# Attention keys turned by their own products, in a two-layer hybrid decoder trunk

## The chip, the cores and the metric

The kernel runs on one core of one Trainium2 chip. The metric is the time of the whole program on the device, in microseconds (us), as a median of runs. A core has five engines that work side by side and meet at semaphores: PE (matrix products; its weight loads are listed as PEld), DVE (vector), ACT (scalar), POOL (GpSimd) and SP (which here only issues DMAs).

## The reference

A trunk of two layers on 256 tokens of width 1024. Layer 0 mixes tokens with multi-head latent attention, then has a dense SwiGLU; layer 1 has an RG-LRU block, then a top-2-of-8 expert SwiGLU. Only attention is touched. Cut to that:

```python
lat = h @ w_in                                  # 1024 -> 384 + 256 + 32
c_q, c_kv, k_rope = split(lat, [384, 640])
c_q, c_kv = rmsnorm(c_q, q_norm), rmsnorm(c_kv, kv_norm)
q  = (c_q @ w_uq).reshape(B, S, 16, 64 + 32)    # q_nope, q_rope
kv = (c_kv @ w_ukv).reshape(B, S, 16, 64 + 64)  # k_nope, v
q_rope, k_rope = apply_rope(q_rope), apply_rope(k_rope)   # one k_rope for all heads
s = (q_nope @ k_nope.T + q_rope @ k_rope.T) * scale       # per head, causal, blocks of 128 queries
o = softmax(s) @ v                              # then @ w_o, residual, and the rest of the trunk
```

## The kernel before

All products of attention's projections are made in three passes of a split float32 (`hi`: rounded to the fast format, `lo`: the rest): `sh*mh`, `sh*ml`, `sl*mh`, three matmuls for each pair of operands (`product`, L431 to L445). A weight unit of 128 rows lands by DMA in `raw`, ACT makes its `w_hi` (`split_hi`), DVE its `w_lo` (`split_lo`). Tokens lie in two tiles of 128 (`TT` = 2).

*Projections.* The normed latents are turned once to `c_hi`, `c_lo` (latent by token). `up_projection` makes q in six units of (token tile, 512 columns): the turned latents of one token tile are the stationary operand (128x128), 512 columns of weight move. The result lies tokens on partitions; ACT copies it to `q` (`q_copy`). Keys and values come together in eight units in the same way, in the order `KV_ORDER`: one unit has four heads of one token tile, 64 columns of key and 64 of value for each head. Each unit's bank is copied in two instructions, the key columns to `k[:, t, head, 0:64]` and the value columns to `v`; ACT copies units 0 to 5, DVE units 6 and 7. GpSimd rotates the 32 columns `k_rope` of each tile (`rope`, six small instructions a tile), then the queries of tile 0, then copies the rotated key part into all 16 heads of `k`, once a tile. DVE rotates the queries of tile 1.

*Heads.* PE's program runs over 16 heads with stages shifted against each other. In step i it turns head i (`transpose_qk`), makes the scores of head i-1 (two matmuls), turns the probabilities of head i-4 (three transposes) and, every second step, multiplies probabilities by values for two heads (`values`). Units 5, 6 and 7 of keys and values stand in steps 0, 1 and 4 (`UP_BETWEEN`). `transpose_qk` is four transposes into one PSUM bank:

```python
for n, src in enumerate([q[:, 0, h], q[:, 1, h], k[:, 0, h], k[:, 1, h]]):
    mm = pe.transpose(psum[0:QK, h % 2, n * P:(n + 1) * P], src, ident[:])
```

In step i ACT copies the turned head (`qk_copy`, 96 partitions x 512 columns into `qkT`, which lies in `gain_mla`), copies the turned probabilities of head i-4 (`pT_copy`), makes the two exponentials of head i-2 (`exps`, L919), and every second step the high half of an output (`o_high`). DVE normalizes head i-3 (L2053 to L2055: a reciprocal and two scalings), makes the maxima of head i-1 with the mask added (L2044, L2047), and every second step the low half of an output (`o_low`, L2060), which waits for `o_high`. PSUM banks and `qkT` are double, by h % 2; the scores of head h wait for the maxima of head h-2. After the last head the output projection runs, whose first parts are already woven between the last heads; then the dense layer.

The order on each engine is written out by hand, and each engine takes its instructions in that order. The copy helper of ACT is L828, so all its copies carry that line; the three matmuls of `product` are L441 to L443; transposes of heads are L1305, scores L1316 and L1317, transposes of probabilities L1326, values L1341 and L1345.

SP issues all weight loads in one queue; ACT and GpSimd issue a few small DMAs of their own.

## Time and profile before

| | |
|---|---|
| median of 3 runs | 1304.98 us (1304.45 to 1305.43) |
| profiled execution, its own time | 1304.9 us |
| span of the trace | 1303.1 us |
| PE busy | 1298.2 us, 100% of the span |
| DVE busy | 649.2 us, 50% |
| ACT busy | 287.8 us, 22% |
| GpSimd busy | 86.9 us, 7% |
| granted PE clock | 1.00 of full speed |
| attention, from the first latent transposes to the last head | about 23 to 87 us |
| experts (L1663) | 67% of the chain that ended last |

The trace is of one execution. Its span begins with the first instruction and ends with the last; the program's own time holds some 1.8 us more around it. A group "x2" is two instructions in a row, merged; the difference of two start times tells how long the engine was held, which is less than the duration printed, since the end of one instruction overlaps the start of the next. A bracket at the end of a row gives the idle time before it and who ended it.

### The profile page before, as it was taken

What the parts mean: (1) busy time and instruction counts of PE and PEld (TensorE: products, weight loads), DVE (VectorE), ACT (ScalarE), POOL (GpSimd) and SP (SyncE); (2) the same over time, 40 slices, a digit from 0 to 9 for tenths busy, and PEclk for the clock granted to TensorE, in tenths of its full rate; (3) what the DMA queues carried; (4) which work ended last, traced back from release to release, by engine and by line L of the source; (5) the groups of instructions that cost most, each with busy time, mean ns of one, the idle gap of its engine ahead of it and who ended that gap; (6) DMA issues with size and microseconds to landing.
All of it is one profiled execution on the core that took longest, in us unless ns stands there. A gap on an engine that the chain in (4) does not pass through costs nothing.

```text
span 1303.1 us, 25215 instructions
## 1 busy us (share of the span) xinstructions
PE 1298.2 (100%) x10760; PEld 852.5 (65%) x10760; DVE 649.2 (50%) x1471; ACT 287.8 (22%) x432; POOL 86.9 (7%) x116
## 2 busy tenths in 40 slices
PE   9999999999999999999999999999999999999998
PEld 5878888888997444555555555555555555555555
DVE  5888666666887344233433533423343353342436
ACT  4874444433694000010010010001001001000102
POOL 3401111111002110000000000000000000000100
PEclk9999999999999999999999999999999999999999
DMA  8625555556369999999999999999999999999992
GB/s 304 253 105 173 193 192 193 193 193 210 120 249 378 358 416 406 421 409 414 419 408 416 419 420 405 419 419 405 405 420 410 403 420 421 411 413 419 419 411 101
DMA packets 124423, 441.92 MB, mean 339 GB/s; under 512 B 7346, under 2 KB 18052, under 8 KB 109732
## 3 DMA queue, kind: packets, MB, share of 16 engines
q1 hardware_dynamic: 119696, 424.57, 82.5%
q0 software_dynamic: 4560, 15.85, 3.4%
q8 instruction: 81, 1.33, 0.4%
q14 instruction: 18, 0.15, 0.0%
q10 hardware_dynamic: 68, 0.02, 0.0%
HBM read 430.84 MB, written 9.57 MB: 338 GB/s over the span
## 4 chain that ended last, share of the span: by engine, by line
PE 98%; ACT 1%; DMA 1%; SPq 0%; issue 0%; DVE 0%
PE psum L1663 67%; PE psum L441 9%; PE psum L443 8%; PE psum L442 8%; PE psum L1210 1%; PE psum L1669 1%; DMA raw<-in_mla_w_in 1%; PE psum L1317 0%; ACT w_hi L412 0%; PE psum L1305 0%; PE psum L1326 0%; PE psum L1341 0%; PE psum L1316 0%; PE psum L1615 0%; PE psum L1428 0%; PE psum L457 0%
## 5 line engine op out<-in xcount | busy, mean ns | idle before, releaser
L1663 PE MATMUL psum<-raw_more,hT 128*32 128x512 f32 x1656 | 535.7, 592 | 0.0
L1663 PE MATMUL psum<-raw,hT 128*32 128x512 f32 x1032 | 334.6, 592 | 0.0
L1663 PE MATMUL psum<-raw_more,xg_odd 128*32 128x512 f32 x1680 | 245.4, 592 | 0.0
L1663 PE MATMUL psum<-raw_more,xg 128*32 128x512 f32 x1704 | 241.8, 592 | 0.1
L2473 DVE STREAM_TRANSPOSE hT<-hid 32x128 f32<-32x128 f32 x672 | 206.2, 307 | 10.3
L2463 DVE SCALAR_TENSOR_TENSOR hid<-hid,psum 96x512 f32<-96x512 f32 x55 | 37.6, 683 | 302.7 <-PE psum L1663 301.9
L1154 ACT ACTIVATE hid<-psum 96x1024 f32<-96x1024 f32 (+1 forms) x32 | 29.2, 914 | 663.8 <-PE psum L1663 474.2
L1663 PEld LDWEIGHTS psum<-raw_more,hT 128*32 128x32 f32 x1656 | 154.3, 110 | 32.0 <-issue 32.0
L1663 PEld LDWEIGHTS psum<-raw_more,xg_odd 128*32 128x32 f32 x1680 | 84.5, 110 | 98.0 <-issue 98.0
L1663 PEld LDWEIGHTS psum<-raw_more,xg 128*32 128x32 f32 x1704 | 83.4, 110 | 98.2 <-issue 97.8
L1663 PE MATMUL psum<-raw,xg_odd 128*32 128x512 f32 x1008 | 147.7, 592 | 0.0
L1663 PE MATMUL psum<-raw,xg 128*32 128x512 f32 x984 | 144.2, 592 | 0.0
L2450 DVE SCALAR_TENSOR_TENSOR hid<-hid,psum 96x1024 f32<-96x1024 f32 (+1 forms) x32 | 34.7, 1083 | 200.7 <-ACT hid L1154 200.7
L418 DVE TENSOR_TENSOR w_lo<-raw,w_hi 128x2048 fp32r<-128x2048 f32 (+1 forms) x52 | 117.4, 2276 | 26.4 <-ACT w_hi L412 26.4
L412 ACT ACTIVATE w_hi<-raw 128x2048 fp32r<-128x2048 f32 (+1 forms) x60 | 111.4, 1891 | 17.1 <-PE psum L443 16.7
L1663 PEld LDWEIGHTS psum<-raw,hT 128*32 128x32 f32 x1032 | 95.4, 110 | 22.7 <-issue 22.5
L1663 PEld LDWEIGHTS psum<-raw,xg_odd 128*32 128x32 f32 x1008 | 50.7, 110 | 58.8 <-issue 58.8
L441 PE MATMUL psum<-w_hi,xTh_ffn 128*128 128x512 f32 x224 | 87.3, 390 | 0.0
L443 PE MATMUL psum<-w_hi,xTl_ffn 128*128 128x512 f32 x224 | 87.2, 389 | 0.0
L442 PE MATMUL psum<-w_lo,xTh_ffn 128*128 128x512 f32 x224 | 87.2, 389 | 0.0
L1663 PEld LDWEIGHTS psum<-raw,xg 128*32 128x32 f32 x984 | 49.5, 110 | 57.3 <-issue 57.3
L828 ACT ACTIVATE y_main<-psum 32x512 f32<-32x512 f32 x48 | 28.4, 592 | 145.1 <-PE psum L1663 145.1
(368 smaller groups left out, 1352.6 us busy)
## 6 DMA issues: line engine op xcount, KB each, us to landing
raw_more<-in_moe_w_gate SPq DMA_DIRECT2D x71, 1024.0 KB, 18.4
raw_more<-in_moe_w_up SPq DMA_DIRECT2D x70, 1024.0 KB, 18.6
raw_more<-in_moe_w_down SPq DMA_DIRECT2D x69, 1024.0 KB, 17.7
raw<-in_moe_w_down SPq DMA_DIRECT2D x43, 1024.0 KB, 18.0
raw<-in_moe_w_up SPq DMA_DIRECT2D x42, 1024.0 KB, 17.5
raw<-in_moe_w_gate SPq DMA_DIRECT2D x41, 1024.0 KB, 18.3
raw<-in_ffn_w_gate SPq DMA_DIRECT2D x14, 1024.0 KB, 5.2
raw<-in_ffn_w_up SPq DMA_DIRECT2D x14, 1024.0 KB, 5.3
```

Source lines behind the costliest of these rows:

```text
L412: act.activation(w_hi[:, s, 0:width], raw[:, s, 0:width], ACT.Copy).then_inc(hi_done[s], 1)
L418: eng.tensor_tensor(w_lo[:, s, 0:width], raw[:, s, 0:width], w_hi[:, s, 0:width].bitcast(F32), ALU.subtract).then_inc(lo_done[s], 1)
L441: pe.matmul(out_ap, sh, mh, start=first, stop=False, **lone)
L442: pe.matmul(out_ap, sh, ml, start=False, stop=False, **lone)
L443: mm = pe.matmul(out_ap, sl, mh, start=False, stop=last, **lone)
L828: return act.activation(dst, src, ACT.Copy)
L1154: act.activation(hid[:, 0:WIDTH[m] * BANK].rearrange("p (a b) -> p a b", b=BANK), psum[SLOT_ROWS, 0:WIDTH[m]], ACT.Tanh, scale=0.5).then_i ...
L1210: mm = pe.matmul(psum[rows_q, 4 + 2 * t + b, 0:LAT // 2], xT_in[:, a, c0:c0 + 32], unit(raw, s, LAT)[:, a % 3, b * LAT // 2:(b + 1) * LAT ...
L1663: return pe.matmul(psum[rows_q, bank, cols], stationary, moving, start=start, stop=stop, tile_position=(0, rows_q.start), skip_group_check ...
L2450: dve.scalar_tensor_tensor(out=h, in0=h, scalar=1.0, in1=psum[SLOT_ROWS, 0:WIDTH[m]], op0=ALU.add, op1=ALU.mult).then_inc(m_mid, 1)
L2463: dve.scalar_tensor_tensor(out=hid[:, cols], in0=hid[:, cols], scalar=0.5, in1=psum[SLOT_ROWS, BANK_U[h]], op0=ALU.mult, op1=ALU.mult).the ...
L2473: ins = dve.transpose(hT[QUARTERS[to], H_BUF[j], :, QUARTERS[b]].rearrange("p (h r) s -> p h r s", r=2), hid[QUARTERS[b], h * BANK:(h + 1) ...
```

## The change

Keys no longer come with tokens on partitions. A unit of keys takes a 128x128 piece of the key weights (two heads x 64) as the stationary operand and moves the turned latents of both token tiles (256 columns) past it; the product is the turned key of two heads. A PSUM bank holds two such products, four heads. Values come as before, in units of their own of 512 columns. So of the eight units, 0, 1, 6, 7 are keys (12 matmuls of 256 columns each) and 2 to 5 are values (6 of 512). To have key and value columns apart, ACT's and DVE's splits of the two weight units write them reordered, in two instructions of half the width each.

The turned keys are copied to `kT` (heads 4 to 15) and `kT_first` (heads 0 to 3), two copies of 64 partitions x 512 columns a unit: units 0 and 1 by ACT, 6 and 7 by DVE. The rotated part is turned once on PE (`turn_key_rope`, two transposes, before the query unit t = 1, b = 1), copied once by ACT into partitions 64 to 95 of head 0 (`key_rope`, before the last query copy) and spread to the other 15 heads by three DMAs from SBUF to SBUF that ACT issues there. GpSimd's two copies into the heads are gone, and its scratch areas are elsewhere. In the heads PE turns only q, and ACT copies 256 columns in place of 512 to `qT`. The scores wait, for head 0, also for the three DMAs, and for heads 8 and 12 for DVE's copies. Three semaphores are merged with others.

```diff
-                rope(t, kr, kr, 1, areas(t, 1))
+                rope(t, kr, kr, 1).then_inc(roped, 1)
+                pool.wait_ge(roped, t + 1)
...
-            for t in range(TT):
-                pool.tensor_copy(k[:, t, :, NOPE:QK],
-                                 latent[:, t, QR + KVR:LAT].unsqueeze(1).broadcast_to([P, HEADS, ROPE])
-                                 ).then_inc(qk_ready, 1)
...
+            def key_rope():
+                act.wait_ge(c_ps, 2 * TT + 1)
+                copy(kT_first[0][NOPE:QK, 0], psum[0:ROPE, 1, T:2 * T]).then_inc(q_copied, 1)
+                act.wait_ge(q_copied, KEY_ROPE)
+                for dst, n in ((kT_first[0][NOPE:QK, 1:2], 1), (kT_first[1][NOPE:QK], 2), (kT[NOPE:QK], HEADS - 4)):
+                    act.dma_start(dst, kT_first[0][NOPE:QK, 0:1].broadcast_to([ROPE, n, T])
+                                  ).then_inc(x_first_then_rope, 16)
...
+                    if t == TT - 1 and b == 1:
+                        key_rope()
...
-            split_hi(act, mla_use(W_UKV), UKV)
-            split_hi(act, mla_use(W_UKV + 1), UKV)
+            for a in range(KVR // P):
...
+                for w in range(2):
+                    ins = act.activation(keys_first(w_hi, s)[:, w], by_head(raw, s)[:, w], ACT.Copy)
+                ins.then_inc(hi_done[s], 1)
...
-                copy(qkT[0:QK, h % 2, :], psum[0:QK, h % 2, :]).then_inc(qkT_ready, 1)
+                copy(qT[0:QK, h % 2, :], psum[0:QK, h % 2, 0:T]).then_inc(qkT_ready, 1)
...
+            def turn_key_rope():
+                pe.wait_ge(roped, TT)
+                for t in range(TT):
+                    mm = pe.transpose(psum[0:ROPE, 1, T + t * P:T + (t + 1) * P], latent[:, t, QR + KVR:LAT],
+                                      ident[:])
+                mm.then_inc(c_ps, 1)
...
+                if KV_UNITS[n][0] == KEYS:
+                    for e in range(2):
+                        g = 2 * KV_UNITS[n][1] + e
+                        terms = []
+                        for a, (s, _) in enumerate(w_units):
+                            pair = [w[:, s, g * P:(g + 1) * P] for w in (w_hi, w_lo)]
+                            terms.append((pair[0], pair[1], c_hi[:, k0 + a, :], c_lo[:, k0 + a, :]))
...
-                for n, src in enumerate([q[:, 0, h], q[:, 1, h], k[:, 0, h], k[:, 1, h]]):
-                    mm = pe.transpose(psum[0:QK, h % 2, n * P:(n + 1) * P], src, ident[:])
+                for t in range(TT):
+                    mm = pe.transpose(psum[0:QK, h % 2, t * P:(t + 1) * P], q[:, t, h], ident[:])
...
+                    pe.wait_ge(q_copied, 3 * TT + 1)
+                    pe.wait_ge(x_first_then_rope, 16 * 4)
+                if h in (8, 12):
+                    pe.wait_ge(kv_copied_v, KV_COPIED[4 + h // 4])
...
+                pe.matmul(psum[:, 2 + h % 2, P:3 * P], s[:, P:2 * P], keys(h),
                           start=True, stop=True).then_inc(score_ps, 1)
...
+                for e in range(2):
+                    dve.tensor_copy(key_pairs(KV_UNITS[n][1], e),
+                                    psum[e * NOPE:(e + 1) * NOPE, KV_BANKS[n]].rearrange("p (g t) -> p g t", t=T)
+                                    ).then_inc(kv_copied_v, 1)
```

## Rows read from the trace of the kernel before

**Rows 1.** Part 4 of the page: shares of the chain that ended last.

```profile
PE 98%; ACT 1%; DMA 1%; SPq 0%; issue 0%; DVE 0%
```

**Rows 2.** Window 70 to 80 us: PE, PEld, DVE, ACT, POOL busy, clock, DMA.

```profile
70.00:80.00 10.00, 10.00 (x101) 7.85 (x103) 9.13 (x48) 9.96 (x35) 0.00 (x0) 1.00 0.01 2
```

**Rows 3.** PE timeline in the heads: start us, us, line, operation, shapes.

```profile
70.36 0.38 PE L1305 MATMUL psum<-ident,k 128*96 128x128 f32 x2
70.57 0.39 PE L1316 MATMUL psum<-gain_mla 96*128 96x128 f32 x2
...
71.23 0.49 PE L1326 MATMUL psum<-ident,res 128*128 128x128 f32 x3
```

**Rows 4.** ACT timeline in the same pair of heads.

```profile
71.60 0.37 ACT L828 ACTIVATE xTh_mla<-psum 128x256 fp32r<-128x256 f32 x1
71.87 0.58 ACT L828 ACTIVATE gain_mla<-psum 96x512 f32<-96x512 f32 x1
72.34 0.48 ACT L828 ACTIVATE early<-psum 128x384 f32<-128x384 f32 x1
```

**Rows 5.** DVE timeline in the same pair of heads.

```profile
68.57 0.15 DVE L2053 RECIPROCAL res<-res 128x2 f32<-128x2 f32 x1
...
70.23 0.16 DVE L2053 RECIPROCAL res<-res 128x2 f32<-128x2 f32 x1
...
72.00 0.42 DVE L2060 TENSOR_TENSOR xTl_mla<-psum,xTh_mla 128x256 fp32r<-128x256 f32 x1
72.34 0.15 DVE L2053 RECIPROCAL res<-res 128x2 f32<-128x2 f32 x1
```

**Rows 6.** PE timeline, matmuls at an even pace: first and last of two stretches.

```profile
41.07 0.39 PE L441 MATMUL psum<-w_hi,xTh_mla 128*128 128x512 f32 x1
...
46.96 0.39 PE L443 MATMUL psum<-w_hi,xTl_mla 128*128 128x512 f32 x1
...
379.83 0.28 PE L441 MATMUL psum<-xTh_lru,w_hi 128*128 128x256 f32 x1
...
383.91 0.28 PE L442 MATMUL psum<-xTl_lru,w_hi 128*128 128x256 f32 x1
```

**Rows 7.** ACT timeline: last query copy, last copy of v, first turned head.

```profile
40.59 0.60 ACT L828 ACTIVATE q<-psum 128x512 f32<-128x512 f32 x1 [1.44 <-PE psum L443]
...
48.67 0.38 ACT L828 ACTIVATE xn_mla<-psum 128x256 f32<-128x256 f32 x1
48.94 0.59 ACT L828 ACTIVATE gain_mla<-psum 96x512 f32<-96x512 f32 x1
```

**Rows 8.** PE timeline: a query product of tile 1; the first scores.

```profile
36.31 0.39 PE L441 MATMUL psum<-w_hi,xTh_mla 128*128 128x512 f32 x1
...
49.58 0.49 PE L1316 MATMUL psum<-gain_mla 96*128 96x128 f32 x2
```

**Rows 9.** DVE timeline: maxima of head 1, normalizing of head 2.

```profile
53.36 0.29 DVE L2044 CUSTOM_DVE_ANT_0 res<-psum,mask 128x128 f32<-128x128 f32 x1 [0.69 <-PE psum L1317]
...
58.66 0.17 DVE L2053 RECIPROCAL res<-res 128x2 f32<-128x2 f32 x1
```

**Rows 10.** GpSimd timeline: the last step of each key rotation.

```profile
32.17 0.22 POOL L720 TENSOR_TENSOR res<-k,res 128x16 f32<-128x16 f32 x1
...
33.73 2.35 POOL L720 TENSOR_TENSOR res<-k,res 128x16 f32<-128x16 f32 x1
```

**Rows 11.** Issues on the ACT queue; 1 MB loads, median us to landing.

```profile
0.80 0.60 ACTq L832 DMA_DIRECT2D q<-in_norm_mix  x1
1.44 0.25 ACTq L833 DMA_DIRECT2D q<-in_positions  x1
...
raw<-in_mla_w_o SPq DMA_DIRECT2D x4, 1024.0 KB, 9.4
```

**Rows 12.** End of the heads: scores of head 15; normalizing of head 11.

```profile
78.37 0.39 PE L1316 MATMUL psum<-gain_mla 96*128 96x128 f32 x2
...
76.11 0.15 DVE L2053 RECIPROCAL res<-res 128x2 f32<-128x2 f32 x1
```

More of the change, by code:

```diff
@@ L83, in trunk @@
                 xn_mla = sb(s, "xn_mla", [P, TT, D], F32)
+                with ExitStack() as s2:
+                    attn_area = sb(s2, "attn_area", [P, 2 * KT, T], F32)
                 xTh_mla = sb(s, "xTh_mla", [P, KT, T], F32R)
@@ L166, in trunk @@
         xT_in = early[:, 2].rearrange("p (k t) -> p k t", t=T)
-        k_row = k[:, 1].rearrange("p h c -> p (h c)")
-        gain_col, x_sumsq, x_rstd = k_row[:, 0:KT], k_row[:, 8:8 + TT], k_row[:, 12:12 + TT]
+        gain_col, x_sumsq, x_rstd = kT[:, 6, 0:KT], kT[:, 6, 8:8 + TT], kT[:, 6, 12:12 + TT]
+        kT_rest = kT.rearrange("p (g e) t -> p e g t", e=2)
+        kT_first = [attn_area[:, n + 5:n + 7] for n in (KT, 0)]
         rope_scratch = [gain_mla[:, n * 256:(n + 1) * 256].rearrange("p (h c) -> p h c", c=HALF) for n in range(3)]
         gain_rows = q[0:KT, 0].rearrange("p h c -> p (h c)")[:, 2 * P:3 * P]
-        rows = k[:, 0].rearrange("p h c -> p (h c)")[:, 0:P]
+        rows = kT[:, 0, 0:P]
         angle_area = q[:, 1].rearrange("p h c -> p (h c)")
@@ L179, in trunk @@
         rope_area = res[:, 1, LAT:LAT + HEADS * HALF].rearrange("p (h c) -> p h c", c=HALF)
-        qkT = gain_mla.rearrange("p (b n) -> p b n", b=2)
+        qT = gain_mla[:, 0:2 * T].rearrange("p (b n) -> p b n", b=2)
+        rope_areas = [attn_area[:, n + KT - 1].rearrange("p (h c) -> p h c", c=HALF) for n in (0, KT)]
         v = xn_mla
@@ L187, in trunk, with keys, key_pairs @@
         Q_BANKS = [(4, 5, 2), (6, 7, 3)]
-        KV_BANKS = [(0, 4, 6, 6), (1, 5, 7, 7)]
-        KV_ORDER = [(t, b) for b in range(4) for t in range(TT)]
+        KV_BANKS = [0, 1, 4, 5, 6, 7, 6, 7]
+        KEYS, VALUES = 0, 1
+        KV_UNITS = [(KEYS, 0), (KEYS, 1), (VALUES, 0, 0), (VALUES, 1, 0), (VALUES, 0, 1), (VALUES, 1, 1),
+                    (KEYS, 2), (KEYS, 3)]
         KV_SCALAR = 6
+        KV_COPIED = [2, 4, 5, 6, 7, 8, 2, 4]
+        KEY_ROPE = 6
+        def keys(h):
+            return kT[0:QK, h - 4] if h >= 4 else kT_first[h % 2][0:QK, h // 2]
+        def key_pairs(n, e):
+            return kT_rest[0:NOPE, e, 2 * n - 2:2 * n] if n > 0 else kT_first[e][0:NOPE]
         hT_f = xn_ffn[:, 0, 0:4 * P].rearrange("p (a b) -> p a b", b=P)
@@ L706, in _, with rope @@
             pool.wait_ge(trig_ready, 1)
-            def rope(t, src, dst, width, areas):
+            def rope(t, src, dst, width):
                 sin = trig[:, 0, t].unsqueeze(1).broadcast_to([P, width, HALF])
@@ L712, in rope @@
                 x1, x2 = src[:, :, 0:HALF], src[:, :, HALF:ROPE]
-                a, b, c = areas
+                a, b, c = [area[:, 0:width] for area in rope_areas + [rope_area]]
                 pool.tensor_tensor(a, x1, cos, ALU.mult).then_inc(pool_link, 1)
@@ L1289, in _ @@
                         transpose_latents(1)
+                    if t == 1 and b == 1:
+                        turn_key_rope()
                     up_projection(W_UQ, QR // P, 0, Q_BANKS, q_ps, t, b)
             def up_kv(n):
-                up_projection(W_UKV, KVR // P, QR // P, KV_BANKS, kv_ps, *KV_ORDER[n])
+                if n in KV_BANK_FREE:
+                    pe.wait_ge(*KV_BANK_FREE[n])
+                w_units = [mla_use(W_UKV + a) for a in range(KVR // P)]
+                units = dict(enumerate(w_units)) if n == 0 else {}
@@ new lines, in up_kv @@
+                k0 = QR // P
+                if KV_UNITS[n][0] == KEYS:
+                    for e in range(2):
[4 more added lines that the diff above has]
+                            terms.append((pair[0], pair[1], c_hi[:, k0 + a, :], c_lo[:, k0 + a, :]))
+                        marks = {}
+                        if e == 1 and n == len(KV_UNITS) - 1:
+                            marks = {a: used[s] for a, (s, _) in enumerate(w_units)}
+                        elif e == 1:
+                            marks = {len(terms) - 1: kv_ps}
+                        product(pe, psum[:, KV_BANKS[n], e * T:(e + 1) * T], terms, marks=marks,
+                                units=units if e == 0 else {})
+                else:
+                    _, t, b = KV_UNITS[n]
+                    tok = slice(t * P, (t + 1) * P)
+                    terms = []
+                    for a, (s, _) in enumerate(w_units):
+                        vals = [w[:, s, HEADS * NOPE + b * BANK:HEADS * NOPE + (b + 1) * BANK] for w in (w_hi, w_lo)]
+                        terms.append((c_hi[:, k0 + a, tok], c_lo[:, k0 + a, tok], vals[0], vals[1]))
+                    product(pe, psum[:, KV_BANKS[n]], terms,
+                            marks={len(terms) - 1: kv_ps})
@@ L1999, in _ @@
             c_low(1)
-            for n in range(W_UKV, W_O):
-                split_lo(dve, mla_use(n), UKV)
+            for a in range(KVR // P):
+                s, n = mla_use(W_UKV + a)
+                dve.wait_ge(hi_done[s], n)
+                for w in range(2):
+                    ins = dve.tensor_tensor(keys_first(w_lo, s)[:, w], by_head(raw, s)[:, w],
+                                            keys_first(w_hi, s)[:, w].bitcast(F32), ALU.subtract)
+                ins.then_inc(lo_done[s], 1)
             def rope_queries(t):
```

92 lines of the change are left out of this document (45 added, 47 removed).

## The prediction

> **What bounds the kernel now.** I read the chain that ended last first: it is PE for 98% of the span [rows 1]. A change in attention therefore pays in full only if PE is what attention waits for, and attention is where I looked next. In a window over the heads PE is busy throughout, at the full clock, but ACT is busy 9.96 of 10 us and DVE 9.13 [rows 2]. So PE is first by very little, and the question is how soon another engine takes over. The timelines give that. For two heads DVE goes through the reciprocal of one head at 68.57, of the next at 70.23, an `o_low` at 72.00, and the next pair begins at 72.34 [rows 5]. The period of a pair is 72.34 - 68.57 = 3.77 us. The first head took 1.66. The second took 1.77, because its `o_low` waited for ACT's copy of the same bank, which runs 71.60 to 71.97 [rows 4, 5]. `o_low` itself holds DVE 0.34. Without that wait DVE needs 1.66 + 1.66 + 0.34 = 3.66 us a pair, and I see no other gap in it. DVE's instructions in the heads are not touched by the change. The most that a head can win is thus (3.77 - 3.66) / 2 = 0.055 us, whatever PE saves.
>
> **The change, part by part.**
>
> *PE in the heads.* Two transposes of k per head go: they take 70.57 - 70.36 = 0.21 us [rows 3], over 16 heads 3.4 us. The pair falls from 3.77 to about 3.35 on PE. ACT's copy of the turned head shrinks from 512 columns (72.34 - 71.87 = 0.47) to 256 (like the one of 71.60 to 71.87, 0.27) [rows 4], 0.20 a head: 3.37 a pair. Both are now under DVE's 3.66, so DVE sets the pace.
>
> *PE outside the heads.* Key units: 4 units of 12 matmuls at 256 columns in place of 4 of 6 at 512. At an even pace 26 steps lie between 41.07 and 46.96, 0.227 each; 34 steps between 379.83 and 383.91, 0.120 each, and those reload 128 x 128 weights every time too [rows 6]. Thus 48 x 0.120 = 5.76 against 24 x 0.227 = 5.45, +0.3 us, 0.08 a unit; a unit takes 1.44. The two transposes of the rotated key part add 0.21. PE's own balance is 3.4 - 0.3 - 0.2 = 2.9 us.
>
> *The wait for the rotated keys.* PE now turns them before the matmuls that began at 36.31 [rows 8], and in order, so everything behind it on PE would stand. GpSimd's last addition for them ran 33.73 to 36.08: 2.35 us for a step that takes 0.22 next to it at 32.17 [rows 10]. It stood beside a 128x2048 subtraction on DVE, and the change cuts these into two of half the width. Even unchanged it ends 0.2 us before PE needs it. Cost 0; if it slipped, PE would pay 1:1. The Trainium skill ("SBUF — State Buffer", SBUF: two separate sides) says that DVE with two SBUF inputs and GpSimd exclude one another for a whole instruction; the 2.35 agrees, and by it halves of a DVE instruction free GpSimd about 1.2 us sooner. The two GpSimd copies of k's rotated part also go; they ran while PE was busy with the units of k and v, and take nothing off the path.
>
> *ACT before the first head.* Here ACT holds the path: the first scores start at 49.58 [rows 8], right after the copy of turned head 0 that began at 48.94 [rows 7]. Whatever ACT gets more before it, PE gets too.
> - `key_rope`: one copy (0.27), a wait for its own end (0.1, my estimate), and three DMA issues, which on this queue took 0.25 and 0.60 [rows 11]. ACT stood idle 1.44 us before the last query copy at 40.59 [rows 7], and that hides the first 1.44 of it. The sum is 1.1 to 2.2 us; with 0.4 an issue, near the middle, 1.57. Cost +0.1, bounds 0 and +0.75. Queued behind it are the last query copy, the split of W_O, DVE's rotation of the queries, the unit copies: all of the ramp.
> - Copies of units 0 and 1: two of 512 columns each (0.47 [rows 4]) in place of two of 256 (0.27 [rows 7]): 4 x 0.20 = +0.8. The 64 partitions do not shorten them; the row gives time by columns. Units 2, 3, 4: one of 0.47 in place of two of 0.27: 3 x -0.07 = -0.2.
> - The splits in two halves and in pieces of 64 columns: the copies of k and v already read such pieces, and the one of 48.67 to 48.94 takes the 0.27 of a plain copy of 256 columns [rows 4, 7]. Two fixed parts more, about 0.07 each (0.27 less 256 columns at 0.20), hide in the wait for weights and for PE before the query copies. Cost 0, at most +0.15.
> - The copy of head 0: -0.2.
> Sum: 0.1 + 0.8 - 0.2 - 0.2 = +0.5, so the first scores start at 50.1.
>
> *From there to head 2.* PE: scores 0.66 [rows 3], unit 6 1.44, so 52.2. DVE copies it in two of 512 columns. A DVE pass over 256 holds it 0.34; with the same fixed 0.07, 512 take 0.61. It is done at 53.4. Before, it was done sooner and DVE stood until the maxima of head 1 at 53.36 [rows 9]: the idle time swallows this one. Scores 1 are ready at 53.2. Then maxima and normalizing twice, 2 x 1.66, to 56.7; unit 7 (done on PE at about 56.4, from the same steps) copied in 1.22, to 57.95; maxima 0.88: normalizing of head 2 starts at 58.85 against 58.66 [rows 9], +0.2. From here DVE has no idle time.
>
> *DVE's run.* From there to the normalizing of head 11 at 76.11 [rows 12] lie 9 heads and 4 `o_low`: 17.45 us now, 9 x 1.66 + 4 x 0.34 = 16.3 then. It starts at 58.85 + 16.3 = 75.15, 1.0 us sooner; the next one at 76.8.
>
> *PE's last head.* The scores of head 15 started at 78.37 [rows 12], with PE itself late: 2.26 us after DVE's 76.11. Now PE waits for DVE instead: it needs the maxima of head 13, at 76.8, and before it the turning of head 11's probabilities (0.65 of normalizing and about 0.33 of turning after 75.15) and three matmuls of projection with their start (3 x 0.227 + 0.1), to 76.95. That is 1.4 us sooner. Behind it PE is busy without a wait to the end of the projection, and its work there is unchanged: between the turnings of two heads' probabilities it has projection and values for some 1.7 to 2 us, and DVE needs 1.66 to 2.0 a head, so DVE, ahead by then, stays ahead (it has head 12 at 77.45, head 13 at 79.1, head 14 at 81.1). The 1.4 us reach the end, since PE is the chain afterwards.
>
> *Transfers.* 15 heads x 32 KB, issued at 39.5 to 40.7, needed at 50.1. The nearest row is the loads of 1 MB in attention, 9.4 us from issue to landing [rows 11]: landing at 50.1, just in time. I take it as hidden, since these transfers stand on another queue and hold half as much, and the 9.4 holds the queueing of loads behind one another. The row does not exclude a wait, so it is a rival. The Trainium skill ("DMA: Bandwidth & Descriptors", Queues, rings and completion order, and Anatomy of one DMA) lets the DMA engines alternate between queues, with a fixed 2 us; by that an estimate is 2.0 + 0.48 MB at half of 436 GB/s = 4.2 us, landing near 45. No row here shows two queues at once under load.
>
> **Sum.** -1.4 us on the span of 1303.1. The profiled execution took 1304.9 with what lies around it, 0.1 below the median of 1304.98. So 1303.5 on its own time, 1303.6 as a median.
>
> **The rivals.**
> - *PE's saving comes in full.* If DVE's steps pack closer than 1.66 once PE and ACT wait for them, and the ramp's +0.5 is idle time elsewhere, PE's balance of 2.9 us comes off: 1302.0. For: PE is 98% of the chain. Against: DVE's steps wait for one another's results and show no gap. Chance 0.14.
> - *The ramp eats it.* Issues of 0.60 each cost 0.75 in place of 0.1, and the `o_low` wait stays for a part of the pairs (0.11 each, 0.5 over the run): -1.4 + 0.65 + 0.5 = -0.2: 1304.8. For: ACT holds the ramp. Chance 0.19.
> - *The spread rows land late* (the other side). Scores of head 0 wait for the third transfer, in order, with all heads behind. At 50.1 it begins to cost; it undoes the gain from 51.5, and is slower by over 0.2% from 54.1, 13.4 us after the last issue. At 15 us it is 55.7: +5.6 - 1.4 = +4.2, 1309.2. For: 9.4 us for loads then. Against: they queue behind their own kind. Chance 0.08.
> - The forecast: 0.59.
>
> **Numbers.** A measurement here tells about 0.2%, 2.6 us, from no change: 1302.4 and 1307.6. The first rival lies just beyond it, and the low flank of the forecast (bounds 0 in place of +0.1 and a DVE step shorter by 0.05, -0.9 over the run) a little: faster 0.16. Slower is the last rival, 0.08. The rest, 0.76, within. The range goes from the first rival, 1302.0, to 1305.8, which takes in the second and the landing up to 52.3.
>
> **What would show it.** DVE with no idle time between the normalizing of head 2 and head 15, and a pair of heads in 3.66 us; PE's busy share in the same window down to 9 of 10, and ACT's too; the first scores at 50.1 after a wait for ACT, not for a DMA; 256-column key matmuls at 0.120; DVE's copies of units 6 and 7 at 0.6 each; no PE wait at 36.3 for GpSimd. It is wrong if the pair takes 3.77 still (PE or ACT had more hidden work), if scores 0 wait for a transfer, or if key matmuls run slower than those of the later layer.

## The result, and the profile after

The changed kernel takes 1306.94 us (median of 14 executions, 1306.20 to 1309.51) against 1304.84 (1304.29 to 1305.43) before: ratio 1.0018, 95% interval 1.0011 to 1.0025. The forecast was 1303.6 with a range up to 1305.8. The time went up by 2.1 us where 1.4 us less were expected.

The profiled execution spans 1304.7 us against 1303.1. Its attention began earlier, though, which has nothing to do with the change: the first set of latent transposes, ahead of everything that the change touches, is already 0.73 us earlier (22.46 against 23.19), and the second set, which serves as the mark below, stands at 31.64 before and at 30.91 after (PE timelines, before and then after; columns: start us, us, engine, line, operation).

```profile
31.64 0.71 PE L1226 MATMUL psum<-ident,res 128*128 128x128 f32 x5
```

```profile
30.91 0.71 PE L1261 MATMUL psum<-ident,res 128*128 128x128 f32 x5
```

Below, "+17.94" means so many us after this row in the same execution; only such distances are compared between profiles.

First the heads. The window of [rows 2], of the changed kernel:

```profile
70.00:80.00 10.00, 9.87 (x96) 7.29 (x89) 9.23 (x48) 9.15 (x36) 0.00 (x0) 1.00 0.01 2
```

ACT fell from 9.96 to 9.15, PE only to 9.87, with fewer matmuls in it. PE's printed durations overlap, so short gaps do not show in its busy time: from q's transposes to the scores of the same head it now takes 0.45 us once a pair (75.14 to 75.59) where 0.26 is usual (73.89 to 74.15). DVE's timeline, which answers to [rows 5], [rows 9] and [rows 12]:

```profile
52.08 0.29 DVE L2123 CUSTOM_DVE_ANT_0 res<-psum,mask 128x128 f32<-128x128 f32 x1 [2.06 <-PE psum L1390]
...
53.51 1.41 DVE L2112 COPY kT<-psum 64x512 f32<-64x512 f32 x2 [0.47 <-PE psum L467]
54.95 0.29 DVE L2123 CUSTOM_DVE_ANT_0 res<-psum,mask 128x128 f32<-128x128 f32 x1
...
60.75 0.16 DVE L2132 RECIPROCAL res<-res 128x2 f32<-128x2 f32 x1
...
66.06 0.42 DVE L2139 TENSOR_TENSOR xTl_mla<-psum,xTh_mla 128x256 fp32r<-128x256 f32 x1 [0.24 <-ACT xTh_mla L844]
...
70.04 0.16 DVE L2132 RECIPROCAL res<-res 128x2 f32<-128x2 f32 x1
...
73.69 0.15 DVE L2132 RECIPROCAL res<-res 128x2 f32<-128x2 f32 x1
...
77.34 0.15 DVE L2132 RECIPROCAL res<-res 128x2 f32<-128x2 f32 x1
```

A pair of heads takes 73.69 - 70.04 = 3.65 us where it took 3.77, and after head 2 DVE waits once, for 0.24 us. The heads run as forecast. But the row at 52.08 shows DVE idle for 2.06 us before its first maxima, and the normalizing of head 11 stands at +46.43, before at +44.47: 1.96 us late. So the loss is made before the heads. ACT's timeline there, which answers to [rows 7]:

```profile
38.08 0.60 ACT L844 ACTIVATE q<-psum 128x512 f32<-128x512 f32 x1 [1.45 <-PE psum L467]
38.70 0.37 ACT L844 ACTIVATE attn_area<-psum 32x256 f32<-32x256 f32 x1
39.10 1.35 ACTq L889 DMA_DIRECT2D attn_area<-attn_area  x2
40.48 0.62 ACTq L889 DMA_DIRECT2D kT<-attn_area  x1
41.15 0.60 ACT L844 ACTIVATE q<-psum 128x512 f32<-128x512 f32 x1 [2.07 <-issue]
41.64 1.91 ACT L436 ACTIVATE w_hi<-raw 128x2048 fp32r<-128x2048 f32 x1
43.45 1.19 ACT L844 ACTIVATE attn_area<-psum 64x512 f32<-64x512 f32 x2
44.67 1.21 ACT L844 ACTIVATE kT<-psum 64x512 f32<-64x512 f32 x2
45.78 1.91 ACT L436 ACTIVATE w_hi<-raw 128x2048 fp32r<-128x2048 f32 x1
47.71 1.09 ACT L844 ACTIVATE xn_mla<-psum 128x512 f32<-128x512 f32 x2
48.82 1.28 ACT L942 ACT_TABLE_LOAD   x1
...
50.70 0.37 ACT L844 ACTIVATE gain_mla<-psum 96x256 f32<-96x256 f32 x1
```

The last query copy no longer ends an idle time "<-PE" but one "<-issue": ACT's own three DMA issues, 39.10 to about 41.10. It stands at +10.24 against +8.95. From it to the first turned head are 9.55 us against 48.94 - 40.59 = 8.35: the four key copies take 45.78 - 43.45 = 2.33.

PE, which answers to [rows 8], [rows 6] and [rows 12]:

```profile
35.60 0.38 PE L1322 MATMUL psum<-ident,res 128*32 128x128 f32 x2
...
39.92 0.28 PE L465 MATMUL psum<-xTh_mla,w_hi 128*128 128x256 f32 x1
...
42.67 0.28 PE L467 MATMUL psum<-xTh_mla,w_lo 128*128 128x256 f32 x1
...
51.12 0.49 PE L1389 MATMUL psum<-attn_area,gain_mla 96*128 96x128 f32 x2 [2.23 <-ACT gain_mla L844]
...
79.49 0.39 PE L1389 MATMUL psum<-kT,gain_mla 96*128 96x128 f32 x2
```

`turn_key_rope` has no wait. Of the 24 key matmuls of units 0 and 1, 23 steps take 2.75 us, 0.120 each. Then PE is idle for 2.23 us, until ACT has copied turned head 0: the first scores are at +20.21 against +17.94. GpSimd's last key step, as [rows 10], and the transfers, as [rows 11] (KB each, median us from issue to landing):

```profile
32.99 1.28 POOL L744 TENSOR_TENSOR res<-attn_area,res 128x16 f32<-128x16 f32 x1
```

```profile
kT<-attn_area ACTq DMA_DIRECT2D x1, 384.0 KB, 9.9
attn_area<-attn_area ACTq DMA_DIRECT2D x1, 64.0 KB, 6.5
attn_area<-attn_area ACTq DMA_DIRECT2D x1, 32.0 KB, 5.7
```

The last transfer lands at 40.48 + 9.9 = 50.4, only 0.7 us before the first scores.

### The profile page after: what moved, and what is told of

It reads as the page before. It is cut to its first block, busy times and chain, and to the rows that moved or that the text cites. A ratio compares the mean times of both kernels' runs of the same rounds, so it can differ in the third digit from the quotient of the medians.

```text
span 1304.7 us, 25196 instructions
## 1 busy us (share of the span) xinstructions
PE 1296.0 (99%) x10754; PEld 763.2 (58%) x10754; DVE 646.6 (50%) x1473; ACT 286.4 (22%) x431; POOL 84.8 (7%) x114
## 4 chain that ended last, share of the span: by engine, by line
PE 98%; ACT 1%; DVE 1%; issue 0%; ACTq 0%; DVEq 0%
PE psum L1739 67%; PE psum L465 9%; PE psum L466 8%; PE psum L467 8%; PE psum L1245 1%; PE psum L1745 1%; PE psum L1390 0%; PE psum L1399 0%; PE psum L1417 0%; PE psum L1389 0%; PE psum L1231 0%; PE psum L1691 0%; ACT w_hi L436 0%; PE psum L1504 0%; DVE kT L2112 0%
## 5 line engine op out<-in xcount | busy, mean ns | idle before, releaser
L1739 PEld LDWEIGHTS psum<-raw_more,hT 128*32 128x32 f32 x1656 | 146.8, 109 | 122.2 <-issue 122.1
L2552 DVE STREAM_TRANSPOSE hT<-hid 32x128 f32<-32x128 f32 x672 | 203.1, 302 | 10.3
L1739 PEld LDWEIGHTS psum<-raw,hT 128*32 128x32 f32 x1032 | 91.1, 109 | 75.7 <-issue 75.5
L442 DVE TENSOR_TENSOR w_lo<-raw,w_hi 128x2048 fp32r<-128x2048 f32 (+1 forms) x50 | 112.6, 2268 | 26.5 <-ACT w_hi L436 26.4
L436 ACT ACTIVATE w_hi<-raw 128x2048 fp32r<-128x2048 f32 (+1 forms) x58 | 107.6, 1890 | 17.0 <-PE psum L467 16.7
L844 ACT ACTIVATE y_main<-psum 32x512 f32<-32x512 f32 x48 | 28.4, 591 | 145.2 <-PE psum L1739 145.2
```

Of the source, the lines that this page charges most:

```text
L436: act.activation(w_hi[:, s, 0:width], raw[:, s, 0:width], ACT.Copy).then_inc(hi_done[s], 1)
L442: eng.tensor_tensor(w_lo[:, s, 0:width], raw[:, s, 0:width], w_hi[:, s, 0:width].bitcast(F32), ALU.subtract).then_inc(lo_done[s], 1)
L844: return act.activation(dst, src, ACT.Copy)
L1739: return pe.matmul(psum[rows_q, bank, cols], stationary, moving, start=start, stop=stop, tile_position=(0, rows_q.start), skip_group_check ...
L2552: ins = dve.transpose(hT[QUARTERS[to], H_BUF[j], :, QUARTERS[b]].rearrange("p (h r) s -> p h r s", r=2), hid[QUARTERS[b], h * BANK:(h + 1) ...
```

## The experiments

Three theories stood after this. *Ramp*: ACT's issues, and its key copies, which hold it longer than forecast because (so I thought) half of them move data to other partitions, start the heads late. *Landing*: the transfers hold the first scores. *Clock*: PE's idle time before the scores lets its granted clock fall. Each table row below is the median of all executions of one kernel (n of them), the number of executions whose mean clock was under 1.0, PE's idle time before the first scores, and three marks of the profile.

| kernel | us | n, under 1.0 | PE idle | last q copy | first scores | head 11 |
|---|---|---|---|---|---|---|
| before | 1304.84 | 14 | none | +8.95 | +17.94 | +44.47 |
| changed | 1306.94 | 14, 3 | 2.23 | +10.24 | +20.21 | +46.43 |
| SP issues after two loads | 1307.82 | 11, 6 | 2.87 | +9.19 | +20.82 | +48.49 |
| one issue more | 1308.31 | 7, 5 | 2.90 | +10.90 | +20.87 | +48.21 |
| copies stay on their partitions | 1306.51 | 10, 3 | 1.66 | +10.24 | +19.64 | +46.49 |
| landing awaited at head 1 | 1307.12 | 11, 3 | 2.23 | +10.21 | +20.19 | +46.41 |
| SP issues ahead of all loads | 1305.43 | 11, 0 | 1.20 | +9.21 | +19.18 | +45.40 |
| PE's idle time filled | 1306.78 | 11, 0 | 0.45 | +10.22 | +20.19 | +46.41 |
| before, three issues added | 1305.09 | 11, 0 | none | +8.96 | +17.94 | +44.47 |
| SP ahead, copies and splits moved | 1307.03 | 11, 0 | none | +9.19 | +17.79 | +46.45 |
| SP ahead, table load early | 1304.17 | 11, 0 | none | +9.18 | +17.78 | +43.89 |
| before, table load early | 1304.03 | 11, 0 | none | +8.97 | +17.84 | +44.05 |
| changed, table load early | 1307.03 | 11, 5 | 2.29 | +10.23 | +20.27 | +47.20 |
| SP ahead, copies stay | 1304.62 | 11, 0 | 0.63 | +9.21 | +18.61 | +44.31 |

"Head 11" is the normalizing of head 11. The kernel before ran beside each group of four rows: 1304.78, 1304.68 and 1304.75 us (30 to 33 executions, all at a mean clock of 1.0). The interval of each ratio below reaches some 0.9 thousandths, 1.2 us, to either side. Smaller steps between two medians are therefore not shown by the medians; they rest on the marks of the profiles. PE's idle time is that of the one profiled execution.

**Who issues, first try.** The three issues go from ACT to SP, behind its second feed-forward load.

```diff
-                act.wait_ge(q_copied, KEY_ROPE)
-                for dst, n in ...:  act.dma_start(dst, ...)
...
+                if s == 1:
+                    sp.wait_ge(q_copied, KEY_ROPE)
+                    for dst, n in ...:  sp.dma_start(dst, ...)
```

> The changed kernel with the three spreading transfers issued by SP, between its second and third load for the dense layer, in place of ACT. Theory A (ACT's issues hold the ramp: the last query copy moved from 40.59 to 41.15 although PE ran 0.73 us earlier, 1.3 us in all): the first scores come 1.3 us sooner than in the changed kernel, 49.8 in place of 51.1 when the starts are aligned, and the kernel is 1.0 to 1.3 us faster than it, 1305.7. Theory B (the landing of the transfers holds the scores, 9.9 us after issue): the transfers now stand behind the loads of SP's own queue and land no sooner than 49.5 to 51, the first scores stay at about 51 and the kernel at 1306.9.

1307.82 us, ratio 1.0020 (1.0011 to 1.0029). ACT gained what it should: its last query copy is at +9.19. But the scores wait for a DMA (PE timeline; DMA list):

```profile
51.81 0.46 PE L1391 MATMUL psum<-attn_area,gain_mla 96*128 96x128 f32 x2 [2.87 <-DMA kT<-attn_area]
```

```profile
kT<-attn_area SPq DMA_DIRECT2D x1, 384.0 KB, 11.0
```

The landing is thus a second bound, and without ACT's issues it is the first one. The window behind it showed what I had not looked for (PE, PEld, DVE, ACT, POOL busy, clock, DMA):

```profile
52.00:56.00 4.00, 4.00 (x21) 3.82 (x21) 1.24 (x6) 0.70 (x3) 0.00 (x0) 0.57 1.00 384
```

The granted clock fell to its lower level, 1.2 GHz (0.50 of full speed from 53 to 55 us), after the idle 2.87 us, and 256-column key matmuls stood 0.21 us apart (53.29, 53.50, 53.72) where the changed kernel has 0.12.

**One issue more on ACT.** A fourth small transfer of the same rows behind the three.

```diff
+                act.dma_start(gain_mla[NOPE:QK, 3 * T:4 * T], kT_first[0][NOPE:QK, 0]).then_inc(...)
```

> The changed kernel with a fourth, small transfer (32 KB, to a place that nothing reads) issued by ACT behind the three. Theory A: the last query copy and the first scores 0.65 us later, the kernel 0.5 to 0.65 us slower than the changed one, 1307.5. Theory B: 32 KB more move the landing by less than 0.1 us and the scores by nothing: 1306.9.

1308.31 us, ratio 1.0028 (1.0017 to 1.0039). ACT's timeline:

```profile
40.97 0.66 ACTq L891 DMA_DIRECT2D gain_mla<-attn_area  x1
41.68 0.60 ACT L844 ACTIVATE q<-psum 128x512 f32<-128x512 f32 x1 [2.76 <-issue]
```

The last query copy and the first scores both come 0.66 us later: an issue at this place costs its full length. The median rose by 1.37. The rest goes with the clock, low in 5 of 7 executions; the two at full clock took 1307.28 and 1308.20.

**Copies that stay on their partitions.** Odd heads take the keys of even heads, from partitions 0 to 63 (so the scores of odd heads are computed from other heads' keys; the work is the same).

```diff
-                        copy(key_pairs(...), bank[e * NOPE:(e + 1) * NOPE].rearrange(
+                        copy(key_pairs(...), bank[0:NOPE].rearrange(
```

The same edit is made to VectorE's copies.

> The changed kernel, but both key copies of a unit read partitions 0 to 63 of the bank, so that the keys of odd heads are those of the even ones (the output is not the reference's). Theory A with its second part (a copy that moves data to other partitions does not overlap the copies around it: 0.60 a copy on ACT in place of 0.48, 0.72 on DVE in place of 0.61): ACT's two units take 1.9 in place of 2.35 us, DVE's two 1.25 in place of 1.41 each, the first scores 0.45 us sooner, the heads another 0.3 sooner, the kernel 0.5 to 0.8 us faster than the changed one. Rival (64 partitions or the layout of the destination make them slow, or a new bank does): the spacing stays 0.60 and 0.72, the time 1306.9.

1306.51 us, ratio 1.0013 (1.0003 to 1.0022). ACT's timeline:

```profile
43.76 1.06 ACT L844 ACTIVATE attn_area<-psum 64x512 f32<-64x512 f32 x2
44.71 1.07 ACT L844 ACTIVATE kT<-psum 64x512 f32<-64x512 f32 x2
45.66 1.92 ACT L436 ACTIVATE w_hi<-raw 128x2048 fp32r<-128x2048 f32 x1
47.47 1.07 ACT L844 ACTIVATE xn_mla<-psum 128x512 f32<-128x512 f32 x2
```

Four copies take 1.90 us, 0.475 each, which is the 0.47 of the forecast; in the changed kernel 2.33. A single copy is no longer there than here (0.58 to 0.60 in both traces); what is missing is the overlap. Here each starts 0.10 to 0.11 us before the end of the one before it, there 0.02 after it.

And it is not the move to other partitions as such that costs it. In the changed kernel the third copy, at 44.67, reads and writes partitions from 0 on, like the first, and yet starts after the end of the second (43.45 + 1.19 = 44.64). So does the first value copy at 47.71, though it stays on its partitions and a split out of SBUF lies between (45.78 + 1.91 = 47.69); here it overlaps that split (47.47 against 45.66 + 1.92 = 47.58). The split itself overlaps in both. DVE shows the same: its maxima at 54.95 start after the end of the key copies (53.51 + 1.41 = 54.92). What all these late starts share is that the instruction reads PSUM from another partition than the last one that read PSUM on its engine: 64 after 0, or 0 after 64. On ACT there are four such changes before the first head, 0.12 to 0.14 us each. I ran no kernel that copies the lower halves of both units first and then the upper ones, which would test this with half of the changes.

The first scores come 0.57 us sooner, and the median fell by 0.43. The profile has the low clock again, after an idle time of only 1.66 us:

```profile
52.00:56.00 4.00, 4.00 (x22) 3.67 (x21) 2.40 (x10) 2.67 (x9) 0.00 (x0) 0.57 1.00 385
```

**Landing awaited at head 1.** `pe.wait_ge(x_first_then_rope, 16 * 4)` moves from the scores of head 0 to those of head 1, the first that read a spread row.

```diff
-                    pe.wait_ge(x_first_then_rope, 16 * 4)
...
+                if h == 1:
+                    pe.wait_ge(x_first_then_rope, 16 * 4)
```

> The changed kernel with the wait for the three transfers moved from the scores of head 0, which need none of them, to the scores of head 1. Theory A: the transfers had landed by 50.4 in the profile, 0.7 us before the scores, so nothing changes: 1306.9. Theory B (in executions without a profile they land later than that, which would also be the scatter of 1306.2 to 1309.5): the median falls by up to 1 us and the scatter to that of the kernel before, about 1 us from lowest to highest.

1307.12 us, ratio 1.0018 (1.0009 to 1.0027), scores at +20.19 as before the edit, after the same "[2.23 <-ACT gain_mla L844]". As the change stands, the landing holds nothing; and the scatter stays (1306.53 to 1308.42), so it does not come from the landing either.

**SP ahead of all loads.** As the first try, but before SP's first feed-forward load.

```diff
+            sp.wait_ge(q_copied, KEY_ROPE)
+            for dst, n in ...:  sp.dma_start(dst, ...)
             for s in range(SLOTS - 1):
                 load(sp, (s, FFN_BASE + 1), ffn_v[s // 2][0, s % 2, 0])
```

> The three transfers of the rotated part are issued by SP ahead of all of the feed-forward loads, not by ACT; nothing else is changed, and the first scores still wait for their landing. Issuing theory (ACT's three issues, 2.0 us less the gap they fill, cost the ramp 1.3 us): the last q copy and all that follows on ACT come 1.3 us sooner, and as the transfers are no longer behind a full queue they land in 6 to 8 us, about 47 to 48 us into the execution, so that the first scores start near 49.8 us after a comparable start of attention; 1306.9 - 1.3 = about 1305.6 us. Rival, landing: the transfers land as late as with the loads ahead of them (11 us after the issue, as in the run in which SP issued them after two loads), and nothing is gained: 1307 to 1308 us. Clock theory (TensorE's idle time before the first scores, 2.2 us in the changed kernel, makes the granted clock fall in part of the executions): with that idle time under 1.5 us no execution has a mean clock under 1.0, and the executions lie within 1.2 us of one another instead of 3.3.

1305.43 us, 1305.04 to 1305.88; ratio 1.0006 (0.9997 to 1.0015). SP's timeline and the DMA list:

```profile
39.13 1.34 SPq L617 DMA_DIRECT2D attn_area<-attn_area  x2
40.51 0.60 SPq L617 DMA_DIRECT2D kT<-attn_area  x1
```

```profile
kT<-attn_area SPq DMA_DIRECT2D x1, 384.0 KB, 3.9
```

With nothing ahead of it the transfer of 384 KB lands in 3.9 us instead of 9.9 or 11.0. SP now also holds its feed-forward loads back until the rotated part is copied: the first is issued at 41.15, in the changed kernel at 35.38, and from 38 to 44 us the DMA engines are busy for 0.58 of the time instead of all of it. That costs nothing here, for PE waits for no load later. The first scores wait for ACT, 1.03 us sooner than in the changed kernel; head 11 is 1.03 us sooner, and no execution had a low clock. Against the kernel before in the same group (1304.68) 0.75 us of the 2.1 are left.

**PE's idle time filled.** Eight unread 128x128 products before the first scores, 1.78 us of work.

```diff
+                    for _ in range(8):
+                        pe.matmul(psum[:, 2, 3 * P:4 * P], ident[:], ident[:], start=True, stop=True)
```

> The changed kernel with eight matrix products of 128x128 fp32 whose result nobody reads, put on TensorE between the products of the second value tile and the first scores, where it stands idle for 2.2 us. Clock theory: the idle time shrinks to under 1 us, the granted clock stays at 1.0 there in every execution, the executions over 1307.5 us vanish and the median falls by 0.3 to 0.5 us, to about 1306.5 us; the ramp itself is unchanged (first scores near 51.1 us). Rival (the scatter comes from the landing of the transfers, which end only 0.7 us before the first scores): the slow executions stay, 1306 to 1309.5 us, median 1306.9.

1306.78 us, ratio 1.0016 (1.0007 to 1.0025). The clock stayed at 1.0 in all 11 executions. With 3 of 14 and 3 of 11 under 1.0 without the filling, this alone could be chance; the tally of all kernels further down makes idle time of PE the likely cause. But the median moved by 0.16 us only and is still 2.10 above the kernel before in its group, and two executions still took 1308.6 and 1309.0, both at full clock. The profiled one is the latter. Its chain of waits has, at the very start, a load:

```profile
1.26 4.78 DMA raw<-in_mla_w_in
6.08 2.47 PE psum L1245 x16
```

and its second latent transposes at 33.14, 2.2 us later than in the changed kernel's profile. That scatter is made before attention and has another cause, which I did not follow.

**Three issues added to the kernel before.**

```diff
+                        for n in range(3):
+                            act.dma_start(scrap[n], ident[0:32, :]).then_inc(x_first, 16)
```

> The kernel before the change, with three DMA issues added to ACT between its last but one and its last copy of q (32 rows of 512 bytes each, to a DRAM tensor that nobody reads). Issuing theory: the ramp alone costs 3 x 0.65 us less what lies in ACT's idle 1.44 us there, and the heads of this kernel, paced by TensorE at 3.77 us a pair, take none of it back: 0.5 to 1.3 us slower, 1305.3 to 1306.1 us. Rival (the heads absorb a late start, the loss lies elsewhere): 1304.8 us as without them. Clock theory adds: if the idle time of TensorE before the first scores grows past 2 us, some executions show a mean clock under 1.0 and take 1.5 us more.

1305.09 us, ratio 1.0003 (0.9994 to 1.0012), all marks unmoved and the span still 1303.1. The issuing theory had 1305.3 at the least and its rival 1304.8; the time lies between them, but the marks settle it, for there is no late start that the heads could absorb. ACT's timeline:

```profile
38.47 1.27 ACTq L878 DMA_DIRECT2D scrap<-ident  x3
40.51 0.60 ACT L829 ACTIVATE q<-psum 128x512 f32<-128x512 f32 x1 [1.44 <-PE psum L444]
```

These issues took 0.42 us each and need no data that ACT makes: they start with the copy before and end at 39.74, inside the cover. Those of the change take 0.67 and start only after the extra copy has ended. The number of issues is not the price; their start and length against the cover are. Which of the two matters more this run cannot tell, as both differ.

**SP ahead, and the work divided anew.** Units 6 and 7 are copied by ACT in steps 2 and 4 of its loop, W_O's third and fourth split are made in steps 0 and 9. DVE's split of the third W_O unit moves too, from before the heads into step 1, where its first key copies were.

```diff
             for n in range(2):
                 kv_copy(n)
-            split_hi(act, mla_use(W_O + 2))
...
-                    split_hi(act, mla_use(W_O + 3))
+                    split_hi(act, mla_use(W_O + 2))
...
+                if i in (2, 4):
+                    kv_copy(KV_SCALAR + i // 2 - 1)
...
+                if i == 9:
+                    split_hi(act, mla_use(W_O + 3))
...
-            for n in (W_O + 1, W_O + 2):
-                split_lo(dve, mla_use(n))
+            split_lo(dve, mla_use(W_O + 1))
...
                 if i == 1:
-                    kv_copy(KV_SCALAR)
+                    split_lo(dve, mla_use(W_O + 2))
```

> The transfers issued by SP as in the first of these runs, and the work before the first heads divided anew: the copies of the last two key units go from VectorE to ACT (steps 2 and 4 of its loop), and ACT's splits of the third and fourth unit of W_O come later, into steps 0 and 9. If ACT's ramp and VectorE's copies are what the change lost, the first scores start near 49 us and VectorE reaches its steady pace (3.65 us a pair, unchanged) 1.4 us of copies sooner: 2.5 to 3 us faster than the change as it stands, 1304.0 to 1304.5 us, below the kernel before. Rival (ACT becomes the pace of the heads, it has 1.2 us of copies and 1.3 us of splits more in them): no more than the 1.3 us of the issues, 1305.6 us. Rival, landing: 1307 us.

1307.03 us, ratio 1.0018 (1.0009 to 1.0027), outside the forecast and its first rival, and met by the landing rival in number only, for no scores wait for a transfer. The first scores are at +17.79, even sooner than before the change, and it is no use: DVE's waits from 48 to 85 us (line waited, releaser: us in total, times, longest) name the new bound.

```profile
DVE res L2138 <- ACT res L957: 3.3, 3, 1.2
DVE res L2129 <- PE psum L1397: 1.9, 1, 1.9
```

DVE's reciprocals now wait for ACT's exponentials: from the first scores to head 11 it takes 28.66 us where the changed kernel takes 26.22. ACT has too little to spare for two copies and a split more: between the normalizing of heads 2 and 11 of the changed kernel it is busy for 15.13 of 16.59 us, 0.3 us a pair free.

**Table load early.** ACT's load of the Exp table, 1.28 us, moves from 48.8 into ACT's idle 1.45 us after the first copy of the second q tile. Three kernels: with SP ahead, the kernel before, and the changed kernel.

```diff
+                    if t == TT - 1 and b == 0:
+                        act.activation(half[:, 1:2], half[:, 0:1], ACT.Exp)
```

> The transfers of the rotated part issued by SP ahead of its feed-forward loads, and ACT's load of the Exp table (1.28 us, with its one-column Exp) moved from behind the value copies to between the first and the second copy of the second q tile, where ACT waits 1.45 us for TensorE. If what remains of the loss is a late first head (first scores 19.2 us after the second set of latent transposes, 17.9 before the change; VectorE then idle for 1.14 us): the first scores come 1.3 us sooner, VectorE starts on them the moment its two splits end, at about 50.0 us, and the time is 1305.4 - 1.0 = 1304.4 us, a little below the kernel before. Rival (the heads take it back: VectorE, at 3.65 us a pair, has 0.46 us more to wait at its first key copy): 1304.9 us or more.

> The kernel before the change with the same move of the table load. There ACT's table load lies before the first scores too, but VectorE is busy with its splits until 50.9 us and takes the first scores (49.6 us) without a wait: the move should bring nothing, 1304.7 us, or at most 0.3 us, if TensorE, which sets the pace there, runs ahead.

> The changed kernel, ACT issuing the transfers as it does there, with the move of the table load alone. The first scores come up to 1.3 us sooner, at about 49.8 us, if the landing lets them; the transfers landed at 50.4 us, so they hold the scores, and the gain is about 0.7 us: 1306.2 us. Without that hold it would be 1305.6 us.

With SP ahead: 1304.17 us, ratio 0.9996 (0.9987 to 1.0005). DVE takes the first scores without a wait (50.27, the moment its splits end), PE's idle time is gone. The kernel before: 1304.03 us, same ratio and interval; I had expected nothing. There the first scores hardly move (+17.84), but head 11 comes 0.42 us sooner: DVE's wait for the scores of head 1 is 0.33 us where [rows 9] has 0.69. The changed kernel: 1307.03 us, ratio 1.0016 (1.0006 to 1.0025), no gain in the median, and the profile's first scores are no sooner. ACT copies turned head 0 at 49.50, and then PE's timeline and the list of DMAs say:

```profile
51.53 0.46 PE L1390 MATMUL psum<-attn_area,gain_mla 96*128 96x128 f32 x2 [2.29 <-DMA kT<-attn_area]
```

```profile
kT<-attn_area ACTq DMA_DIRECT2D x1, 384.0 KB, 10.6
```

One execution of this kernel took 4456.58 us; it is unexplained, and without it the median is 1306.8. The other ten fall in two groups: five at full clock, 1305.6 to 1306.6, five below it, 1307.0 to 1309.5. The profiled one is of the second group. The median of the first, 1305.72, is 1.06 below that of the changed kernel at full clock (1306.78), so where the clock stays up the move does gain; no trace shows whether the transfers land sooner there.

**Both at once.** SP ahead and copies that stay on their partitions (odd heads again with even heads' keys).

> The transfers issued by SP ahead of its feed-forward loads, and all key copies reading partitions 0 to 63 of their bank (odd heads get the keys of even heads), so that no copy moves data to other partitions. If the move across partitions costs its 0.12 us a copy on ACT and 0.08 on VectorE beside the issues and not in their place: first scores 0.6 us sooner than with the SP issues alone, VectorE's four copies 0.3 us shorter together, 1305.4 - 0.7 = about 1304.7 us. If not (the copies' cost was in part that of the late q copy): 1305.2 us.

1304.62 us, ratio 0.9999 (0.9990 to 1.0008). First scores at +18.61, 0.57 us sooner than with SP ahead alone; DVE's copies take 0.60 us each instead of 0.72; head 11 at +44.31, 1.09 sooner. The 0.57 is what the copies gave back without SP's issues too, so the two costs add.

## Why the prediction was wrong

**Step that failed: ACT before the first head.** The scores were to come 0.5 us later and came 2.27 later.
- `key_rope` was put at +0.1 (bounds 0 and +0.75). Measured +1.29 at the last query copy. The mechanism, ACT's extra work less its idle time, was right, the size was off: copy and wait took 39.10 - 38.70 = 0.40 (forecast 0.37), but the three issues 41.15 - 39.10 = 2.05 (forecast 1.2), more than three times the longer row of [rows 11]. 2.45 less the cover of 1.44 leaves 1.01, and moving the issues away gives back 1.03. The other 0.26 (9.21 - 8.95) is the turning inside the query products, which I had booked in PE's balance and not in the ramp.
- Key copies were put at 0.47 each by a row whose copies overlap their neighbours. The second copy of each unit reads PSUM from partition 64, and with the partition changing from copy to copy the overlap is gone: the four take 2.33 us instead of 1.88 (+1.28 for +0.8), and the first value copy behind them comes another 0.12 late. Value copies (-0.20 for -0.2) and the shorter copy of head 0 (-0.22 for -0.2) were right.

These are the whole of it: 1.29 + 1.28 + 0.12 - 0.20 - 0.22 = 2.27 us.

**From there to head 2.** 60.75 - 51.12 = 9.63 us against 8.75 forecast, +0.88. DVE's copies of units 6 and 7 were put at 0.61 and take 0.72 each, 0.60 where all start at partition 0: +0.44. DVE starts the first pair 2.39 us after the first scores (53.51) and not 2.1, as the sum counted PE's last product by its step of 0.12 and not by its printed 0.28: +0.29. The second pair waits 0.17 for unit 7 in the same way. The late scores are not behind it: with the scores on time (SP ahead, table load early) the same stretch takes 9.53 us.

**DVE's run.** 3.65 us a pair, forecast 3.66: right, and so is that DVE sets the pace and PE's saving of nearly 3 us is not seen. The sign that PE's busy share would fall to 9 of 10 did not come (9.87). Head 2 to head 11 took 16.59 for 16.3, of which 0.24 is one `o_low` wait. The end, normalizing head 11 to the scores of head 15, took 2.15 for 1.8.

In sum 1.77 + 0.88 + 0.29 + 0.35 = 3.29 us, and -1.4 became +1.85 at the scores of head 15. PE then carries it on, with no wait that the kernel before does not have: its last group of matmuls, at 1298.12 against 1296.94, is 1.91 late by the mark. The two profiles differ by another 0.42 us behind that group, which is open.

**Right:** no PE wait for GpSimd, whose last step took 1.28 us in place of 2.35 and ended 1.1 us sooner by the common mark; the Trainium skill ("SBUF — State Buffer", SBUF: two separate sides) gave about 1.2 for it, and the trace agrees. Key matmuls at 0.120. The transfers: taken as landing at 50.1 by the loads' 9.4 us, they landed at 50.4. The estimate from the Trainium skill ("DMA: Bandwidth & Descriptors", Queues, rings and completion order, and Anatomy of one DMA), 4.2 us, does not hold with loads queued ahead or beside (9.9 to 11.0). The 3.9 with nothing ahead lies near it, but by luck in part: the estimate halved the rate for loads that share the engines, and there were none. The fixed 2 us of the Trainium skill ("DMA: Bandwidth & Descriptors", Anatomy of one DMA) is, besides, a fit over transfers that GpSimd issues, and these are issued by ACT and SP. The rival in which they hold the scores was false for the change as it stands and true 0.7 us away from it, as two experiments show. The rival "the ramp eats it" named the right place; it stopped at 0.75 us for what cost 1.29, of which the issues made 1.03.

**Not foreseen: the clock.** It is not the main cause: 11 of 14 executions of the changed kernel had full clock, with a median of 1306.78, and filling the idle time left 1306.78. It adds its share on top where the idle time is long: none of 55 executions of the five variants with 1.20 us of idle time or less, 3 of 10 at 1.66, 3 of 14 and 3 of 11 at 2.23, 5 of 11 at 2.29, 6 of 11 at 2.87, 5 of 7 at 2.90. Within the last group, which ran side by side, it is 5 of 11 at 2.29, and 0 of 22 in the two changed kernels with 0.63 or none. The filling is the only run that changes the idle time alone; the rest is argued from this tally. Between the medians of a kernel's executions at lowered and at full clock lie 1.0 to 2.4 us.

**What the edit is worth without ACT's late start.** Both kernels with the table load early, and SP ahead for the new one: 1304.17 and 1304.03, no difference that this measurement can tell. By the marks the new one is 0.71 us behind at head 2 (+27.31 against +26.60) and takes 16.58 us from there to head 11 where the old one takes 17.45. Taking k's transposes off PE thus buys 0.87 us in nine heads and loses 0.71 before them. The key copies' lost overlap is still in this figure; a kernel without it as well, with the table load early, was not run.

## What to carry to other kernels

Before work is taken off the busiest engine, look at the engine that starts the stage: here each us that ACT lost before the first head was lost at head 11 too, and only 0.12 us a pair came back. A DMA issue is work of its engine; lay its start and length, and those of the copy it waits for, into the idle row that is to cover it. Issue a small transfer ahead of the large loads, not behind them. And when a copy's price is taken from a row, look whether it overlapped its neighbours there, and whether it will here.

## What the runs showed of the hardware

- An issue of an SBUF-to-SBUF transfer with 32 rows held ACT's or SP's queue for 0.60 to 0.69 us; one of 16 KB from SBUF to DRAM 0.42.
- A copy of 64 partitions x 512 columns from PSUM, in a run of them: 0.475 us each on ACT where all read from partition 0, 0.58 on average where they read from 0 and 64 in turn; on DVE 0.60 and 0.72. A copy alone is printed equally long in both cases (0.58 to 0.60 on ACT, 0.67 to 0.69 on DVE); in the second no copy overlaps the one before, and neither does the next instruction that reads PSUM from partition 0.
- The same 384 KB transfer landed after 3.9 us with nothing ahead, after 9.9 and 10.6 with loads on the other queue, and after 11.0 behind two loads on its own.
- PE's granted clock fell from 2.4 to 1.2 GHz after idle times of 1.66 to 2.90 us, in some executions and not in others of the same kernel.
